# Index-score products of a sparse attention sent in fours over four PSUM banks instead of in twos over two

## The chip, the cores and the metric

The kernel runs on one core of one Trainium2 chip. The metric is the device time of one execution in microseconds (us); lower is better. The engines are TensorE (PE; PEld is its weight load), VectorE (DVE), ScalarE (ACT), GpSimd (POOL) and SyncE (SP, which only issues DMAs). They run their own instruction streams in order and meet at semaphores.

## The reference

One decoder layer on 512 tokens of width 2048 in float32: retention heads beside sparse attention, then an MLP, with norms and conditioning around them. The change touches only the indexer of the sparse attention, which scores every key for every query and keeps the best 128:

```python
h = _modulate(_rms_norm(x, norm1_g), shift1, scale1)
proj = h @ w_in                      # rq, rk, rv, rg, dq, dk, dv, iq, ik, iw
...
s = jnp.einsum('bqhd,bsd->bqhs', qib, k_idx)            # 16 index heads of 64, one shared key
score = jnp.einsum('bqhs,bqh->bqs', jax.nn.relu(s), wb)  # weighted sum over the heads
score = jnp.where(causal, score, -jnp.inf)
_, idx = lax.top_k(score, topk)
```

The query is taken in blocks of 128 tokens. Block 0 needs no choice. Blocks 1, 2 and 3 see 256, 384 and 512 keys.

## The kernel before

**Chunks.** Every large product of the layer is a stream of chunks, numbered q. A chunk is 24 TensorE products of 128 rows by 512 columns (`product`, L1196; three products of split operands for each of eight places). Its weights come by DMA in units of four chunks. ScalarE writes the high half of a chunk's weights (`w_hi`, L514) and GpSimd the low half (`w_lo`, L739), four chunks ahead. Chunks 24 to 27 are `features_chunk`, whose rows read `pj<-h,w_hi` (the moving operand is named first); from chunk 28 on they are `tokens_chunk`, whose rows read `pj<-w_hi,h` and which goes through four token blocks `tb`, six products each.

**Index items.** There are 48 items, one for each query block (1, 2, 3) and index head; items 0 to 23 are the first eight heads, 24 to 47 the last eight. Eight items in a row have the same width: 256, 384, 512 columns, then again. Item n is worked on by three engines in turn:

- TensorE: one small product of 64 rows (L1413, `pa<-ikT,iqT`; the trace shows two weight loads and two matmuls for each) into bank n % 4 of the PSUM tensor `pa`. Even heads lie in partitions 0 to 63 and odd ones in 64 to 127.
- ScalarE: relu out of the bank into one of two halves of the SBUF tile `stage` (`index_relu`, L606). It waits until item n - 2 has been added, since that used the same half.
- VectorE: multiplies by the head's weight and adds to `score` (`index_item`, L924 for head 0 of a block and L927 for the others).

**Where the items stand.** `INDEX_ITEMS` says how many items go with chunk 24, 25, and so on, up to chunk 33: 6, 6, 6, 6, 4, 4, 4, 4, 4, 4. On TensorE they stand inside the chunk, in twos: in a features chunk behind the second, fourth and seventh of its eight places; in a tokens chunk behind the first and the third token block. A two waits until the item four places before its second one has been taken out of its bank (`need(pe, idx_taken, n - 2)`).

**What else runs there.** On VectorE the items of chunk q stand ahead of a piece of another job, `ada_add` (L1013 and L1015: four linked operations of 512 columns on rows that a DMA brings; the accumulator is `part_rows` or `ada_acc`). From chunk 30 on rounds of the top-k search (L937, L938) stand between. On ScalarE the relus of chunk q + 1 stand behind the split of chunk q + 4 and, in chunks 24 to 27, behind the copy of an `iqT` tile (L550) that the last eight heads need (`iq_ready`). After chunks 26 and 30 TensorE sums an accumulator (`later_mod`, L1276); the one after chunk 30 goes to bank 3 of `pa` and so waits for all items that have been sent.

Of the kernel before, what the change touches and what calls it, by code (L numbers as in the profile page):

```python
# [82 lines left out]
Q_TOPK = 30  # L83
ROUNDS = (2, 2, 2, 2, 3, 4, 3, 3, 2, 3, 3, 3, 3, 3, 3, 3, 4)
Q_INDEX = 24
INDEX_ITEMS = (6, 6, 6, 6, 4, 4, 4, 4, 4, 4)

Q_ADA = 16
ADA_SUMS = 16
# [12 lines left out]
def need(eng, sem, value):  # L102

    if isinstance(value, int) and value <= 0:
        return
    eng.wait_ge(sem, value)
# [20 lines left out]
def build(nc, x, vecs, b_ada, consts, w_ada, w_in, w_out, w_mlp1, w_mlp2, out):  # L127
    base = 16512

    def at(name, offset, shape, dt=F32):  # L130
        return nc.alloc_sbuf_tensor_at(name, shape, dt, offset=base + offset)
# [17 lines left out]
    def small(name, *shape):  # L149
# [46 lines left out]
    first = [at("ada_first0", 12 * 4096, [P, 2048]), at("ada_first1", 14 * 4096, [P, 2048]),  # L196
             at("ada_first2", RC + 4096, [P, 2048]), at("ada_first3", RC + 22528, [P, 2048])]
# [51 lines left out]
    iq_ready, idx_done, idx_taken = sem("iq_ready"), sem("idx_done"), sem("idx_taken")  # L249
# [63 lines left out]
    def span(i):  # L313
        return P * (i + 1)
# [15 lines left out]
    def items_at(q):  # L330
        m = q - Q_INDEX
        return range(sum(INDEX_ITEMS[:m]), sum(INDEX_ITEMS[:m + 1])) if 0 <= m < len(INDEX_ITEMS) else ()

# [28 lines left out]
    with block:  # L362
# [829 lines left out]
        def _(pe):  # L1192
            def product(dst, lhs, rhs, start, stop):

                for n, (a, b) in enumerate(PASSES):
                    last = pe.matmul(dst, lhs[a], rhs[b], start=start and n == 0, stop=stop and n == 2)  # L1196
                return last
# [4 lines left out]
            def tokens_chunk(u, j, k0, is_first, is_last, freed, count, items=()):  # L1202

                pe.wait_ge(lo_done, 4 * u + j + 1)
                for tb in range(NB):
                    if is_first and j == 0 and freed is not None:
                        pe.wait_ge(freed, count + tb + 1)
                    for kk in range(2):
                        kt = k0 + 2 * j + kk
                        cols = slice(512 * kk, 512 * kk + 512)  # L1210
                        last = product(pj[:, tb, :], [h[:, kt, s, P * tb:P * tb + P] for s in (HI, LO)],
                                       [w_hi[:, j, cols], w_lo[:, j, cols]],
                                       is_first and j == 0 and kk == 0, is_last and j == 3 and kk == 1)
                    if is_last and j == 3 and tb < 3:
                        last.then_inc(proj_done, 1)
                    if tb == NB - 1:
                        last.then_inc(chunk_used, 1)
                    if tb % 2 == 0:
                        for n in items[tb:tb + 2]:
                            index_item(n)  # L1220

            def tokens_pair(u, freed, count):
# [13 lines left out]
            def features_chunk(q, src, k0, bank, start, stop, ready=None, count=0, trip=0, items=()):  # L1236

                j = q % 4
                pe.wait_ge(lo_done, q + 1 + 32 * trip)
                for kk in range(8):  # L1240
                    if ready is not None:
                        pe.wait_ge(ready, count + kk + 1)
                    last = product(bank, [w[:, j, P * kk:P * kk + P] for w in (w_hi, w_lo)],
                                   [src[:, k0 + kk, s, :] for s in (HI, LO)], start and kk == 0, stop and kk == 7)
                    if kk == 7:
                        last.then_inc(chunk_used, 1)
                    if kk in (1, 3, 6):
                        first = 2 * (1, 3, 6).index(kk)
                        for n in items[first:first + 2]:
                            index_item(n)  # L1250


# [149 lines left out]
            def index_item(n):  # L1402
                i, hh = ITEMS[n]
                rows = slice(IDX_DIM * (hh % 2), IDX_DIM * (hh % 2) + IDX_DIM)
                if n == 0:
                    pe.wait_ge(ikT_ready, 1)
                    pe.wait_ge(kT_ready, KV)
                if n % 4 == 3:
                    pe.wait_ge(mod_taken, done["bank3"])
                if n % 2 == 0:  # L1410
                    need(pe, idx_taken, n - 2)
                pe.wait_ge(iq_ready, 4 if n < 24 else 8)
                pe.matmul(pa[:, n % 4, 0:span(i)], iqT[rows, hh // 2, P * i:P * i + P], ikT[rows, 0:span(i)],  # L1413
                          start=True, stop=True).then_inc(idx_done, 1)
                done["items"] += 1


            for q in range(Q_IQ, Q_LOOP):
                hf, j = divmod(q - Q_IQ, 4)
                if q == Q_IQ + 3:  # L1420
                    pe.wait_ge(small_taken, 1)
                features_chunk(q, h, 8 * hf, pj[:, j, :], hf == 0, hf == 1, items=items_at(q))
                if q == Q_IQ:
                    pe.wait_ge(small_taken, 1)
                    for tb in range(NB):
                        last = pe.transpose(pa[:, 0, P * tb:P * tb + SMALL], small_rows[0:SMALL, P * tb:P * tb + P],
                                            con[0:SMALL, C_ID:C_ID + SMALL])
                    last.then_inc(small_turned, 1)
                if q == Q_IQ + 2:
                    pe.wait_ge(ik_ready, 8)  # L1430
                    pe.wait_ge(proj_free, 8)
                    for tb in range(NB):
                        last = turn(pa[:, 0, P * tb:P * tb + P], ik2[:, tb].rearrange("p a b -> p (a b)"))
                    last.then_inc(ik_turned, 1)
                for n in ada_sum_at(q):
                    later_mod(n)
# [45 lines left out]
            for q in range(Q_LOOP, Q_WO):  # L1482
                g, r = divmod(q - Q_LOOP, PER_GQ)
                group, hf = r // 8, r % 8 // 4

                if group == 0:
                    freed, count = (v_taken, 4 * g - 4) if g else (iq_ready, 4)
                else:
                    freed, count = proj_free, 8 + 16 * g + 4 * (group - 1)
                if q == Q_LOOP:  # L1490
                    pe.wait_ge(mod_taken, done["mods"])
                if r in (24, 32):
                    tokens_pair(q // 4, freed, count)
                elif r not in (25, 33):
                    tokens_chunk(q // 4, q % 4, 8 * hf, hf == 0, hf == 1, freed, count, items_at(q))
                if r == Q_TURN_AT:
                    q_transposes(g)
                if r in TURNS_AT:
                    p_transposes(4 * g + TURNS_AT.index(r))
                if r in OUTS_AT:  # L1500
                    head_out(4 * g + OUTS_AT.index(r))
                if r in LOGITS_AT:
                    head_logits(4 * g + LOGITS_AT.index(r))
                for n in ada_sum_at(q):
                    later_mod(n)
# [60 lines left out]
            for r in range(32):  # L1566
                half_, t = divmod(r, KT)
                if r == KT:
                    last_head_pair()
                if r in (KT, KT + 1):  # L1570
                    continue
                if r >= 4:
                    pe.wait_ge(added, r - 3)
                if r < 4:
                    pe.wait_ge(v_taken, 4 + r + 1)
                features_chunk(4 * U_WO + r, h, 8 * half_, pj[:, t % 4, :], True, True,
                               yd_ready if r == 0 else None)
                if r < 16:
                    k, odd = divmod(r, 2)
                    if not odd:  # L1580
                        if k > 0:
                            ret_out(k - 1)
                        need(pe, yr_ready, k - 1)
                        ret_turn(k)
                    else:
                        ret_inner(k)
                        if k > 0:
                            ret_back(k - 1)
                if r == 15:
                    ret_out(7)  # L1590
# [136 lines left out]
```

## Time and profile before

| | us |
|---|---|
| median of 3 runs | 2377.06 |
| lowest and highest | 2375.36, 2377.11 |
| the profiled execution, own time | 2375.35 |
| its span in the trace | 2373.5 |

The profile's page shows each engine's busy time over the span, the span in 40 slices, the chain of work that ended last, and the costliest groups of instructions. The index items lie between 201 and 286 us, about one part in 28 of the span.

### The profile page before, as it was taken

The numbers are of one execution on the slowest core, as the hardware profiler recorded it, in microseconds if no ns is written. First come the engines' busy times: TensorE is split into PE (matmuls) and PEld (weight loads), VectorE is DVE, ScalarE is ACT, GpSimd is POOL, SyncE is SP. The second block draws the span as 40 slices with busy tenths as digits, with TensorE's granted clock in tenths as the row PEclk, the third lists the DMA queues.
The fourth block names the chain that finished last, engine by engine and source line by source line (L and its number), as shares of the span: only waits on it lengthen the run. The fifth ranks groups of instructions, "written<-read, shape, count | busy, mean of one in ns | idle before, by whom it ended". The sixth has DMA issues, their size and how long they took to land.

```text
span 2373.5 us, 26660 instructions
## 1 busy us (share of the span) xinstructions
PE 2343.3 (99%) x10778; PEld 1902.1 (80%) x10778; DVE 964.1 (41%) x1360; ACT 644.1 (27%) x891; POOL 973.7 (41%) x414
## 2 busy tenths in 40 slices
PE   7999999999999999999999999999999999999999
PEld 4676688788878888788888888888888888888887
DVE  2249898877876877621121121121121121121121
ACT  4223332323224221321221221221221221221222
POOL 1343343344334334344444444444444444444442
PEclk9999999999999999999999999999999999999999
DMA  9976464578647423222333233223323322332231
GB/s 379 357 278 230 161 211 143 196 273 293 223 146 270 142 89 107 71 107 76 102 107 95 82 106 106 85 92 106 106 73 103 106 98 78 106 106 84 93 129 49
DMA packets 183985, 342.13 MB, mean 144 GB/s; under 512 B 4417, under 2 KB 31332, under 8 KB 183012
## 3 DMA queue, kind: packets, MB, share of 16 engines
q1 hardware_dynamic: 175280, 336.77, 41.4%
q10 hardware_dynamic: 8628, 4.28, 0.6%
q8 instruction: 55, 0.90, 0.2%
q14 instruction: 22, 0.18, 0.0%
HBM read 324.26 MB, written 16.78 MB: 144 GB/s over the span
## 4 chain that ended last, share of the span: by engine, by line
PE 93%; DVE 3%; DMA 2%; ACT 1%; issue 0%; SPq 0%; POOL 0%; ACTq 0%; DVEq 0%
PE pj L1196 56%; PE pa L1196 31%; DMA ada_first<-w_ada_in 2%; PE pa L1200 1%; PE pa L1283 1%; DVE part_rows L1015 1%; PE pa L1454 1%; PE pa L1413 1%; PE pa L1477 1%; DVE h L834 1%; PE pa L1276 1%; DVE relu L830 0%; PE pa L1534 0%; PE pa L1526 0%; DVE score L927 0%
## 5 line engine op out<-in xcount | busy, mean ns | idle before, releaser
L739 POOL TENSOR_TENSOR w_lo<-raw,w_hi 128x1024 fp32r<-128x1024 f32 (+1 forms) x396 | 954.5, 2412 | 1339.9 <-ACT w_hi L514 1339.8
L514 ACT ACTIVATE w_hi<-raw 128x1024 fp32r<-128x1024 f32 (+1 forms) x396 | 416.1, 1054 | 1491.2 <-PE pj L1196 945.7
L1196 PE MATMUL pj<-h,w_hi 128*128 128x512 f32 (+1 forms) x1696 | 526.0, 391 | 2.1 <-POOL w_lo L739 1.6
L1196 PE MATMUL pj<-w_hi,h 128*128 128x512 f32 x1408 | 454.1, 396 | 2.2 <-DVE h L834 1.1
L1196 PEld LDWEIGHTS pj<-h,w_hi 128*128 128x128 f32 (+1 forms) x1696 | 314.6, 187 | 74.5 <-issue 7.2
L1196 PE MATMUL pa<-h,w_hi 128*128 128x512 f32 x1152 | 354.9, 389 | 0.0
L1196 PE MATMUL pj<-h,w_lo 128*128 128x512 f32 (+1 forms) x848 | 330.2, 389 | 0.0
L1196 PEld LDWEIGHTS pj<-w_hi,h 128*128 128x128 f32 x1408 | 264.4, 188 | 74.4 <-issue 14.4
L1196 PE MATMUL pa<-mid,w_hi 128*128 128x512 f32 x1024 | 316.1, 390 | 0.0
L1196 PE MATMUL pj<-mid,w_hi 128*128 128x512 f32 x1024 | 315.8, 390 | 0.0
L1196 PE MATMUL pj<-w_lo,h 128*128 128x512 f32 x704 | 274.4, 390 | 0.0
L1196 PEld LDWEIGHTS pa<-h,w_hi 128*128 128x128 f32 x1152 | 216.2, 188 | 45.0
L1196 PE MATMUL pa<-h,w_lo 128*128 128x512 f32 x576 | 224.1, 389 | 0.0
L1196 PEld LDWEIGHTS pj<-mid,w_hi 128*128 128x128 f32 x1024 | 191.8, 188 | 39.6
L1196 PEld LDWEIGHTS pa<-mid,w_hi 128*128 128x128 f32 x1024 | 191.6, 188 | 39.5
L1196 PE MATMUL pa<-mid,w_lo 128*128 128x512 f32 x512 | 199.3, 389 | 0.0
L1196 PE MATMUL pj<-mid,w_lo 128*128 128x512 f32 x512 | 199.3, 389 | 0.0
L1196 PEld LDWEIGHTS pj<-h,w_lo 128*128 128x128 f32 (+1 forms) x848 | 158.5, 187 | 34.1
L1183 DVE SCALAR_TENSOR_TENSOR resid<-pa,mod,resid 128x512 f32<-128x512 f32 x64 | 48.1, 751 | 304.0 <-PE pa L1196 304.0
L1183 DVE SCALAR_TENSOR_TENSOR resid<-pj,mod,resid 128x512 f32<-128x512 f32 x64 | 47.5, 751 | 276.8 <-PE pj L1196 276.8
L1196 PEld LDWEIGHTS pj<-w_lo,h 128*128 128x128 f32 x704 | 132.3, 188 | 27.4 <-issue 1.7
L1015 DVE SCALAR_TENSOR_TENSOR ada_acc<-ada_rows,csilu,ada_acc 128x512 f32<-128x512 f32 x120 | 132.4, 1103 | 25.9 <-DMA ada_rows<-w_ada_in 22.0
(177 smaller groups left out, 1689.5 us busy)
## 6 DMA issues: line engine op xcount, KB each, us to landing
raw<-w_mlp_in SPq DMA_DIRECT2D x64, 2048.0 KB, 8.5
ada_rows<-w_ada_in SPq DMA_DIRECT2D x64, 1024.0 KB, 5.3
raw<-w_in_in SPq DMA_DIRECT2D x22, 2048.0 KB, 10.0
ada_first<-w_ada_in SPq DMA_DIRECT2D x32, 1024.0 KB, 10.9
raw<-w_out_in SPq DMA_DIRECT2D x8, 2048.0 KB, 8.6
ret<-ret_dram SPq DMA_DIRECT2D x32, 256.0 KB, 3.9
raw<-w_in_in SPq DMA_DIRECT2D x3, 1792.0 KB, 13.0
x_nat<-x_in SPq DMA_DIRECT2D x4, 1024.0 KB, 10.4
```

What stands on the lines that cost most here:

```text
L514: act.activation(split_chunk(w_hi, u, j), raw_chunk(u, j), ACT.Copy).then_inc(hi_done, 1)
L739: pool.tensor_tensor(split_chunk(w_lo, u, j), raw_chunk(u, j), split_chunk(w_hi, u, j).bitcast(F32), ALU.subtract).then_inc(lo_done, 1)
L834: dve.scalar_tensor_tensor(h[:, kt, LO, :], tmp[:, kt % 2, :], mod[:, shift_col + kt:shift_col + kt + 1], h[:, kt, HI, :].bitcast(F32), AL ...
L1015: last = dve.scalar_tensor_tensor(acc[:], ada_rows[b][:, i, :], c_col, acc[:], ALU.mult, ALU.add)
L1183: dve.scalar_tensor_tensor(resid[:, t, :], (pa if v % 2 else pj)[:, j, :], mod[:, 5 * KT + t:5 * KT + t + 1], resid[:, t, :], ALU.mult, AL ...
L1196: last = pe.matmul(dst, lhs[a], rhs[b], start=start and n == 0, stop=stop and n == 2)
L1200: return pe.transpose(dst, src, ident)
L1276: last = pe.matmul(bank[:, m:m + 1], rows[:, P * m:P * m + P], ones[:, 0:1], start=True, stop=True)
L1283: last = pe.matmul(pa[32 * i:32 * i + 32, 3, :], c_wide[:, at_:at_ + 32], src[i], start=sec == 0 and s == 0, stop=sec == 1 and s == 3)
L1413: pe.matmul(pa[:, n % 4, 0:span(i)], iqT[rows, hh // 2, P * i:P * i + P], ikT[rows, 0:span(i)], start=True, stop=True).then_inc(idx_done, 1)
L1454: last = pe.matmul(pa[:, bank, col:col + span(i)], qT[:, j, P * i:P * i + P], kT[:, g, 0:span(i)], start=True, stop=True)
L1477: last = pe.matmul(pa[:, 3, P * kb:], v_nat[:, kb, P * g:P * g + P], pT[:, PT_AT[kb]:PT_AT[kb] + width], start=kb == 0, stop=kb == NB - 1, ...
```

## The change

`INDEX_ITEMS` becomes 4, 8, 4, 8, 4, 4, 4, 4, 4, 4. Items are sent in fours: in a tokens chunk all four behind the first token block; in a features chunk with four items behind the fourth place, and in one with eight items behind the second and the sixth place. Since a four fills all four banks, its first item now waits until every item before it has been taken (`need(pe, idx_taken, n)`), and the other three no longer wait for banks.

```diff
-INDEX_ITEMS = (6, 6, 6, 6, 4, 4, 4, 4, 4, 4)
+INDEX_ITEMS = (4, 8, 4, 8, 4, 4, 4, 4, 4, 4)
...
-                    if tb % 2 == 0:
-                        for n in items[tb:tb + 2]:
+                    if tb == 0:
+                        for n in items:
                             index_item(n)
...
-                    if kk in (1, 3, 6):
-                        first = 2 * (1, 3, 6).index(kk)
-                        for n in items[first:first + 2]:
+                    if len(items) == 8 and kk in (1, 5):
+                        for n in items[kk - 1:kk + 3]:
+                            index_item(n)
+                    if len(items) == 4 and kk == 3:
+                        for n in items:
                             index_item(n)
...
-                if n % 2 == 0:
-                    need(pe, idx_taken, n - 2)
+                if n % 4 == 0:
+                    need(pe, idx_taken, n)
```

On TensorE in chunk 25, before: the last two items of 256 columns (6 and 7), four rows of the chunk's products, and the first two of 384 columns (8 and 9).

```order
L1413 MATMUL pa<-ikT,iqT 128x256 x2
L1196 MATMUL pj<-h,w_hi 128x512 x2
L1196 MATMUL pj<-h,w_lo 128x512
L1196 MATMUL pj<-h,w_hi 128x512 x2
L1196 MATMUL pj<-h,w_lo 128x512
L1413 MATMUL pa<-ikT,iqT 128x384 x2
```

The same place after the change: items 4 to 7, four places of products, items 8 to 11.

```order
L1415 MATMUL pa<-ikT,iqT 128x256 x4
L1196 MATMUL pj<-h,w_hi 128x512 x2
L1196 MATMUL pj<-h,w_lo 128x512
L1196 MATMUL pj<-h,w_hi 128x512 x2
L1196 MATMUL pj<-h,w_lo 128x512
L1196 MATMUL pj<-h,w_hi 128x512 x2
L1196 MATMUL pj<-h,w_lo 128x512
L1196 MATMUL pj<-h,w_hi 128x512 x2
L1196 MATMUL pj<-h,w_lo 128x512
L1415 MATMUL pa<-ikT,iqT 128x384 x4
```

Two items stand together where four do now, and twice as many products lie between one group and the next.

On VectorE, in chunks 24 and 25 (the scores of 256 columns, then the `ada_add` of chunk 24 on `part_rows`, then the scores of chunk 25), with - for before and + for after:

```order
 L924 TENSOR_SCALAR score<-stage,w_idx 128x256
-L927 SCALAR_TENSOR_TENSOR score<-stage,w_idx,score 128x256 x5
+L927 SCALAR_TENSOR_TENSOR score<-stage,w_idx,score 128x256 x3
 L1013 TENSOR_SCALAR part_rows<-ada_rows_77,csilu 128x512
 L1015 SCALAR_TENSOR_TENSOR part_rows<-ada_rows_77,csilu,part_rows 128x512 x3
-L927 SCALAR_TENSOR_TENSOR score<-stage,w_idx,score 128x256 x2
+L927 SCALAR_TENSOR_TENSOR score<-stage,w_idx,score 128x256 x4
```

The scores of items 4 and 5 stood ahead of the `ada_add` and now stand behind it.

## Rows read from the trace of the kernel before

**Rows 1.** The page: busy time, share of the span, instructions.
```profile
PE 2343.3 (99%) x10778; PEld 1902.1 (80%) x10778; DVE 964.1 (41%) x1360; ACT 644.1 (27%) x891; POOL 973.7 (41%) x414
```

**Rows 2.** Waits between 200 and 290 us: total, times, longest.
```profile
ACT stage L606 <- DVE score L927: 28.8, 19, 4.2
PE pa L1413 <- ACT iqT L550: 1.1, 1, 1.1
```

**Rows 3.** Chain that ended last, around 237 us: start, us, what.
```profile
218.10 0.76 DVE part_rows L1015
...
234.97 0.76 DVE score L927
...
235.82 0.60 ACT stage L606
...
237.26 0.59 ACT iqT L550
...
237.99 0.70 PE pa L1413 x4
```

**Rows 4.** Timeline of TensorE: start, us, operation, [idle before <- releaser].
```profile
200.31 0.39 PE L1196 MATMUL pj<-h,w_lo 128*128 128x512 f32 x1
...
200.99 0.39 PE L1196 MATMUL pj<-h,w_lo 128*128 128x512 f32 x1
201.30 0.70 PE L1413 MATMUL pa<-ikT,iqT 64*128 64x256 f32 x4
201.94 0.72 PE L1196 MATMUL pj<-h,w_hi 128*128 128x512 f32 x2
202.50 0.40 PE L1196 MATMUL pj<-h,w_lo 128*128 128x512 f32 x1
...
211.55 0.92 PE L1413 MATMUL pa<-ikT,iqT 64*128 64x384 f32 x4
212.40 0.72 PE L1196 MATMUL pj<-h,w_hi 128*128 128x512 f32 x2
...
227.56 1.13 PE L1413 MATMUL pa<-ikT,iqT 64*128 64x512 f32 x4
228.62 0.73 PE L1196 MATMUL pj<-h,w_hi 128*128 128x512 f32 x2
...
258.82 1.02 PE L1276 MATMUL pa<-con,part_rows 128*128 128x1 f32 x8 [0.16 <-issue]
```

**Rows 5.** Timeline of TensorE, narrow products of another job, several in a row.
```profile
69.32 1.07 PE L1283 MATMUL pa<-ada_first,c_wide 128*32 128x512 f32 x8
...
90.88 1.93 PE L1283 MATMUL pa<-ada_first,c_wide 128*32 128x512 f32 x16
...
110.80 3.64 PE L1283 MATMUL pa<-ada_first,c_wide 128*32 128x512 f32 x32
```

**Rows 6.** Timeline of VectorE.
```profile
206.40 0.35 DVE L924 TENSOR_SCALAR score<-stage,w_idx 128x256 f32<-128x256 f32 x1
206.85 2.84 DVE L927 SCALAR_TENSOR_TENSOR score<-stage,w_idx,score 128x256 f32<-128x256 f32 x5
209.60 0.48 DVE L1013 TENSOR_SCALAR part_rows<-ada_rows,csilu 128x512 f32<-128x512 f32 x1
...
214.43 1.07 DVE L927 SCALAR_TENSOR_TENSOR score<-stage,w_idx,score 128x256 f32<-128x256 f32 x2
...
227.31 5.12 DVE L1015 SCALAR_TENSOR_TENSOR part_rows<-ada_rows,csilu,part_rows 128x512 f32<-128x512 f32 x4
232.34 0.15 DVE L808 TENSOR_TENSOR mod<-pj,bias_cols 128x4 f32<-128x4 f32 x1
232.41 5.03 DVE L927 SCALAR_TENSOR_TENSOR score<-stage,w_idx,score 128x512 f32<-128x512 f32 x6
...
274.85 1.61 DVE L927 SCALAR_TENSOR_TENSOR score<-stage,w_idx,score 128x512 f32<-128x512 f32 x2 [2.15 <-ACT stage L606]
```

**Rows 7.** Timeline of ScalarE.
```profile
207.43 0.39 ACT L606 ACTIVATE stage<-pa 128x256 f32<-128x256 f32 x1 [0.21 <-DVE score L927]
...
208.60 0.39 ACT L606 ACTIVATE stage<-pa 128x256 f32<-128x256 f32 x1 [0.20 <-DVE score L927]
```

**Rows 8.** Stretches: us, busy time by engine, granted clock, DMA share, GB/s.
```profile
10.00:20.00 10.00, 5.90 (x46) 2.75 (x44) 1.71 (x10) 5.22 (x9) 0.00 (x0) 1.00 1.06 393
20.00:30.00 10.00, 7.18 (x33) 5.45 (x34) 0.00 (x0) 5.02 (x7) 0.00 (x0) 0.53 1.02 402
60.00:70.00 10.00, 7.76 (x45) 4.47 (x49) 0.00 (x0) 0.40 (x1) 3.07 (x2) 1.00 1.05 387
290.00:345.00 55.00, 55.00 (x260) 45.97 (x259) 52.53 (x105) 21.46 (x54) 26.85 (x11) 1.00 0.45 155
```

## The prediction

> **What bounds the kernel now.** I first read the busy times of the page: TensorE works for 99% of the span [rows 1]. So any time that the change takes off TensorE's stream, or puts into it, is time of the kernel, unless another engine takes it back. Then I read the waits in the stretch of the index items. TensorE stands still only once there for another engine's copy, 1.1 us before item 24 [rows 2]. ScalarE's relus, though, wait 28.8 us in 19 pieces for VectorE's scores. The chain that ended last says why this matters: from 218 to 238 us it hardly touches TensorE. It runs over VectorE's `ada_add` and its scores, the last relus of items 20 to 23, the copy of the `iqT` tile, and only then TensorE's item 24 at 237.99 [rows 3]. VectorE works there with hardly a gap from 206.4 us on [rows 6]. So two engines are near the limit in this stretch: TensorE, and VectorE a little behind it. TensorE passes only because it is allowed to run ahead of VectorE by up to four items.
>
> **What a two costs, and what a four would.** Three products of 512 columns take 0.68 us (200.31 to 200.99), 0.228 each. From the product at 200.99 to the one at 202.50 are 1.51 us with three products and one two of 256 columns: the two costs 1.51 - 0.68 = 0.83 us. Of that the two itself holds 0.64 us (201.30 to 201.94); the other 0.19 us are a late start and a slow first product behind it. A two of 384 columns holds 0.85 us and one of 512 holds 1.06 us [rows 4]; with the same 0.19 they cost 1.04 and 1.25. Eight of each: 8 x (0.83 + 1.04 + 1.25) = 25.0 us.
>
> The trace of before shows no four of this shape. The slope of the three rows is 0.42 us for 256 columns; a second two that simply streams on would add its columns alone: 0.43, 0.64, 0.85 us. The nearest row that has several groups in a row is the narrow product of the conditioning job: 8 matmuls last 1.07 us, 16 last 1.93, 32 last 3.64, so each further group of 512 columns adds 0.86 us [rows 5]. This agrees with 0.85, so I take it. A four then gives back 0.40 us over two twos, and twelve fours give back 12 x 0.40 = **4.8 us** (bounds: 0 if the second two pays as much as the first, 12 x 0.4 if it streams on).
>
> **What the new wait costs.** A four waits until every earlier item is out of its bank. An item is out when ScalarE has done its relu, and that needs the score of the item two before. I went through the stretch with these steps: relu 0.39 us at 256 columns [rows 7] and some 0.5 and 0.6 at 384 and 512; score 0.57, 0.70, 0.84 us from one to the next (2.84/5; 5.03/6); `ada_add` 4.8 to 5.1 us (209.60 to 214.43; 5.12) [rows 6].
>
> First stop, chunk 25. Chunk 24 starts at 199.85 (six products before 201.30). It holds 24 products and one four (0.83 + 0.43), so it ends at 206.6, 1.2 us earlier than before because two items less are in it. Items 4 to 7 come 6 products later at 208.1; item 3 was taken at 207.8 [rows 7], so no wait. The four costs 1.26 us less its lead-in, twelve products 2.74, and TensorE wants items 8 to 11 at 212.0. VectorE has scored items 0 to 3 at 208.5. Its `ada_add` follows at once and lasts to 213.5. Only then comes the score of item 4 (to 214.1), which lets relu 6 go; after the score of item 5, relu 7 goes at 214.7 and is done at 215.1. TensorE stands still for **3.1 us**. Before, items 8 and 9 needed only that item 5 was out of its bank, which it was at 209.0 [rows 7], 2.5 us ahead of them [rows 4].
>
> Second stop, chunk 27, the same with 512 columns. TensorE wants items 20 to 23 at 232.3. VectorE has got back part of its lag and ends the `ada_add` of chunk 26 at 231.8; the scores of 16 and 17 and the relu of 19 end at 233.9: **1.6 us**.
>
> Third stop, item 24 in chunk 28. It exists already, 1.1 us [rows 2, 3]. The relus of items 20 to 23 start only when the late four is in its banks; VectorE ends its scores some 1.7 us later than before, and the `iqT` copy comes at 239.7 instead of 237.9. But TensorE too is later and wants it at 238.9: **0.8 us**, 0.3 less than before.
>
> In the tokens chunks 28 to 33 a four stands behind the first six products, one whole chunk (7 us) after the last. Items 28 and 32 are wanted at about 246.6 and 253.4, and the relus before them end 0.5 and 0.0 us earlier: no wait, but nothing to spare at the second. What is late next is the sum behind chunk 30, which takes bank 3 and waits for items 34 and 35. Before it waited 0.16 us [rows 4]. Now VectorE ends the `ada_add` of chunk 29 at about 258.3, relu 35 ends at 260.3, and TensorE wants the bank at 259.1: **1.2 us**. Behind it the `w_hi` and `w_lo` work is four chunks ahead and hides there. SyncE's queue keeps its order; its loads of `ada_rows` and weights wait for VectorE and GpSimd by at most the same 2 us, and no wait of TensorE in this stretch is for them.
>
> **The sum.** Saved: 4.8. New stops: 3.1 + 1.6 + (0.8 - 1.1) + (1.2 - 0.2) = 5.4. Net **+0.6 us**. The same hand calculation run on the order of before gives TensorE's rows to 0.3 us throughout, so I trust its differences to about 1 us. If the second two in a four saved nothing, three of the stops would shrink to 2.5, 1.0 and 0.5 us and the last would be gone, and the net would be about +1.5. The stops give way where TensorE is slower; that is what it means that VectorE sets the pace. Against the profiled execution's own 2375.35 us the sum is 2376.0; the median of the runs shown lies 1.7 higher, at 2377.06, and gives **2377.6**.
>
> The Trainium skill bears on this from two sides. TensorEngine Tiling (Array Packing), Key Properties, says that changing the tiling mode drains TensorE, which is the 0.40 us that a four saves; by that rule alone the time would be 2372.3. The same page, under PSUM Bottleneck, says that tiling speeds up TensorE but not the emptying of PSUM, which may become the bottleneck. By that rule the gain stays with the engines that empty the banks, and the 28.8 us of relus waiting for scores already show it here.
>
> **The rivals.**
>
> A: *the gain comes through.* If the fours seldom waited, 4.8 us would go, 2377.06 - 4.8 = 2372.3. For it: every item's wait is satisfied early from chunk 31 on, where VectorE waits up to 2.15 us for relus [rows 6]. Against it: at chunk 25 the order on VectorE puts a 5 us `ada_add` between the scores of items 3 and 4, whatever the exact durations. To come out at 0, that wait would have to end 3 us sooner. And behind the items VectorE is busy 52.5 of 55 us up to 345 [rows 8], so it would take back part of an early arrival. Half a gain (2374 to 2375) is likelier than the whole.
>
> B: *the stop costs the clock.* TensorE's granted clock fell to 0.53 in the stretch from 20 to 30 us, the level of 1.2 GHz, after a stretch in which it was busy 5.9 of 10 us; after 7.76 busy of 10 it stayed at 1.00 [rows 8]. In the new kernel some 3.1 us of idle come in one piece near 212 us. If the clock then fell for as long as it did there, products would take twice as long for some 10 us and 5 us would be lost: 2377.6 + 5 = 2382.6, slower. It decides only if the stop at 212 us is as good as the sparse work ahead of 20 us; against it speaks that the stretch from 60 us has 2.2 us of idle and kept its clock, and that TensorE is full on both sides of the stop. The Trainium skill, in TensorE: Matmul & The Clock Gate (Why this matters for your kernels), warns of the clock falling back after an idle gap between bursts of matmuls, so the risk is to be counted.
>
> C: *the fours do not run as one.* The weight loads of the second two wait for the first, nothing is saved, and the stops remain: +1.5 to +2 us, 2378.8. The narrow products speak against it.
>
> **How the numbers follow.** The forecast, stops and savings that nearly cancel (-1.5 to +2.5 us), has 0.72. C has 0.10. A has 0.08 in its full form and 0.04 in the half form. B has 0.06. Faster or slower by 0.2% means below 2372.3 or above 2381.8; about so much can be told from no change by a measurement of this kernel. A's full form lies at the edge, so faster gets 0.06. Slower gets B and a small part for stops that are longer than I think, 0.09. The same: 0.85. The range takes the forecast, the half form of A and C, and the scatter of 1.7 us that the runs of before show: 2374.2 to 2380.6.
>
> **What would show it.** In the trace after: L1415 with 8 matmul rows together, lasting about 1.1, 1.6 and 2.0 us; TensorE idle some 3 us before item 8 near 212 us, 1.6 near 232, under 1 near 239, and about 1 before the sum after chunk 30; 48 items ended at about the same time as before, near 282 us; TensorE's clock at 1.00 there. The forecast is wrong if the wait near 212 is under 2 us with the others gone (A), or if the clock row there is under 1 (B). It would also be wrong if something behind 290 us moved by more than 1 us, which I do not expect.

## The result, and the profile after

| | before | after |
|---|---|---|
| median, us | 2376.76 (6 runs) | 2394.88 (6 runs) |
| lowest and highest | 2375.36, 2377.11 | 2391.32, 2397.76 |
| profiled execution, own time | 2375.35 | 2397.76 |
| its span | 2373.5 | 2396.0 |

The change makes the kernel slower: 1.0074 times before, with an interval of 1.0064 to 1.0085. That is 18.1 us where 0.6 were forecast, far outside the range of 2374.2 to 2380.6.

The page of the kernel after: the busy time of the engines, and the queue that brings the instructions (packets, MB, share of the DMA engines' span). The first row answers to [rows 1]; the queue's row in the page of before is 55 packets and 0.90 MB.

```profile
span 2396.0 us, 26649 instructions
PE 2351.9 (98%) x10778; PEld 1913.1 (80%) x10778; DVE 953.5 (40%) x1360; ACT 644.0 (27%) x891; POOL 977.0 (41%) x414
q8 instruction: 100, 1.64, 0.3%
```

TensorE has as many matmuls as before, 8.6 us more busy time and 22.5 us more span. So it stands still more, and runs slower in places. The waits of TensorE between 200 and 290 us, in the kernel after (total, times, longest), beside [rows 2]:

```profile
PE pa L1415 <- ACT stage L606: 4.1, 2, 2.7
PE pa L1278 <- ACT stage L606: 1.4, 1, 1.4
PE pa L1415 <- ACT iqT L550: 0.7, 1, 0.7
PE pa L1415 <- DVE mod L808: 0.6, 1, 0.6
```

The first three rows are the four stops of the prediction. The last one was not in it. But all this is 6.8 us of standing still, against 1.3 in before, and the fours save 4.8 of work. The larger part of the 22.5 us is far away, in the MLP. Its steps are a loop in TensorE's own stream: six passes, with a jump back after each of the first five. The waits of TensorE between 1000 and 2390 us, in the kernel after:

```profile
PE pj L1196 <- issue: 8.5, 5, 2.0
```

The kernel before has no such row there. "Issue" is time in which the engine waits for nothing that the profile shows. The timeline of TensorE in the kernel after, around the first and the third of the five stops (start, duration, what, [idle before <- releaser]):

```profile
1324.52 0.61 PE L1196 MATMUL pj<-h,w_hi 128*128 128x512 f32 x2
1324.97 0.39 PE L1196 MATMUL pj<-h,w_lo 128*128 128x512 f32 x1
1325.20 0.39 PE L1196 MATMUL pj<-h,w_hi 128*128 128x512 f32 x1
1327.27 0.50 PE L1196 MATMUL pj<-h,w_hi 128*128 128x512 f32 x1 [1.69 <-issue]
1327.61 0.39 PE L1196 MATMUL pj<-h,w_lo 128*128 128x512 f32 x1
...
1679.18 0.51 PE L1196 MATMUL pj<-h,w_hi 128*128 128x512 f32 x1 [1.75 <-issue]
1679.52 0.40 PE L1196 MATMUL pj<-h,w_lo 128*128 128x512 f32 x1
1679.75 0.62 PE L1196 MATMUL pj<-h,w_hi 128*128 128x512 f32 x2
1680.22 0.41 PE L1196 MATMUL pj<-h,w_lo 128*128 128x512 f32 x1
1680.44 1.03 PE L1196 MATMUL pj<-h,w_hi 128*128 128x512 f32 x2
1681.27 0.63 PE L1196 MATMUL pj<-h,w_lo 128*128 128x512 f32 x1
```

Four products of a chunk are issued and then nothing for 1.7 us, and no wait for weights, operands or banks shows. This comes once behind each of the five jumps. Behind the third stop a pair of products soon lasts 1.03 us instead of 0.61: the clock has fallen. The stretch of 3.4 us there (busy of PE, PEld, DVE, ACT, POOL, then the granted clock, DMA share, GB/s):

```profile
1680.00:1683.40 3.40, 3.40 (x10) 2.67 (x9) 0.00 (x0) 0.00 (x0) 0.00 (x0) 0.57 0.64 176
```

So the 22.5 us of the two spans divide into:

- the part with the loop, from one and the same product (the 4667th matmul of the trace, at 998 us here and at 991 in before) to the last small products of the output: 15.2 us (five stops, 8.5; three stretches of 3.4 us at half clock, at 1680.5, 1857.9 and 2035.4 us, which lose 1.7 each; the remaining 1.6 are not taken apart),
- the index section, from the first product of chunk 24 to the 876th product (L1196) of the trace, near 310 us: 111.86 us instead of 109.02, so 2.84,
- 4.5 us elsewhere: chunk 24 starts 2.8 us later, before any changed row, and one stretch at half clock lies near 967 us. Both come and go in the profiles of other kernels below, whatever their order of items.

### The profile page after: what moved, and what is told of

The parts are those of the page before. It is cut to its first block, busy times and chain, and to the rows that moved or that the text cites. A ratio compares the mean times of both kernels' runs of the same rounds, so it can differ in the third digit from the quotient of the medians.

```text
span 2396.0 us, 26649 instructions
## 1 busy us (share of the span) xinstructions
PE 2351.9 (98%) x10778; PEld 1913.1 (80%) x10778; DVE 953.5 (40%) x1360; ACT 644.0 (27%) x891; POOL 977.0 (41%) x414
## 3 DMA queue, kind: packets, MB, share of 16 engines
q8 instruction: 100, 1.64, 0.3%
## 4 chain that ended last, share of the span: by engine, by line
PE 91%; DVE 5%; DMA 2%; issue 1%; ACT 0%; SPq 0%; POOL 0%; ACTq 0%; DVEq 0%
PE pj L1196 54%; PE pa L1196 31%; DVE part_rows L1015 1%; DMA ada_first<-w_ada_in 1%; DVE ada_acc L1015 1%; PE pa L1200 1%; PE pa L1285 1%; DMA ada_rows<-w_ada_in 1%; PE pa L1456 1%; DVE score L927 1%; PE pa L1479 1%; DVE h L834 0%; DVE relu L830 0%; PE pa L1278 0%; DMA rows<-vecs 0%
## 5 line engine op out<-in xcount | busy, mean ns | idle before, releaser
L1196 PE MATMUL pj<-h,w_hi 128*128 128x512 f32 (+1 forms) x1696 | 530.8, 394 | 10.5 <-issue 8.5
L1196 PE MATMUL pj<-w_hi,h 128*128 128x512 f32 x1408 | 454.4, 397 | 1.8 <-DVE rot L965 1.4
L1196 PEld LDWEIGHTS pj<-h,w_hi 128*128 128x128 f32 (+1 forms) x1696 | 317.1, 188 | 83.4 <-issue 15.1
L1196 PE MATMUL pa<-h,w_hi 128*128 128x512 f32 x1152 | 355.0, 389 | 0.0
L1196 PE MATMUL pj<-h,w_lo 128*128 128x512 f32 (+1 forms) x848 | 332.0, 392 | 0.0
L1196 PEld LDWEIGHTS pj<-w_hi,h 128*128 128x128 f32 x1408 | 265.8, 189 | 71.7 <-issue 12.5
L1196 PE MATMUL pa<-mid,w_hi 128*128 128x512 f32 x1024 | 316.2, 390 | 0.0
L1196 PE MATMUL pj<-mid,w_hi 128*128 128x512 f32 x1024 | 315.9, 390 | 0.0
L1196 PE MATMUL pj<-w_lo,h 128*128 128x512 f32 x704 | 275.6, 392 | 0.0
L1196 PEld LDWEIGHTS pa<-h,w_hi 128*128 128x128 f32 x1152 | 216.2, 188 | 45.1
L1196 PE MATMUL pa<-h,w_lo 128*128 128x512 f32 x576 | 224.1, 389 | 0.0
L1196 PEld LDWEIGHTS pj<-mid,w_hi 128*128 128x128 f32 x1024 | 191.9, 188 | 39.6
L1196 PEld LDWEIGHTS pa<-mid,w_hi 128*128 128x128 f32 x1024 | 191.6, 188 | 39.5
L1196 PE MATMUL pa<-mid,w_lo 128*128 128x512 f32 x512 | 199.3, 389 | 0.0
L1196 PE MATMUL pj<-mid,w_lo 128*128 128x512 f32 x512 | 199.3, 389 | 0.0
L1196 PEld LDWEIGHTS pj<-h,w_lo 128*128 128x128 f32 (+1 forms) x848 | 159.7, 188 | 34.5
L1196 PEld LDWEIGHTS pj<-w_lo,h 128*128 128x128 f32 x704 | 133.1, 189 | 27.8 <-issue 1.7
L1015 DVE SCALAR_TENSOR_TENSOR ada_acc<-ada_rows,csilu,ada_acc 128x512 f32<-128x512 f32 x120 | 126.9, 1058 | 30.2 <-DMA ada_rows<-w_ada_in 26.4
```

The lines of the kernel that those rows point to most:

```text
L1015: last = dve.scalar_tensor_tensor(acc[:], ada_rows[b][:, i, :], c_col, acc[:], ALU.mult, ALU.add)
```

## The experiments

Two questions: what stops the loop, and why the index section costs 2.8 us and not 0.6. Unless it is said otherwise a ratio is against the kernel before, run on the same chip.

**What stops the loop.** The one thing that the change moves there is the place of the code. Half of the bank waits of the items went, from 22 instructions to 11, and TensorE's stream has 14,240 instructions instead of 14,251; the page's total went from 26,660 to 26,649. The instructions come in packets of 16 KB (1.64 MB in 100). Theory: a packet is a piece of code, TensorE keeps a few pieces, and where the loop's start lies among their edges decides if the loop stays or must be fetched again in each pass. Rival: the fours in the index section do it, by something that they leave behind.

**e1, the fours with the code at its old place.** The missing waits are put back behind the fours' first wait, where they are met at once.

```diff
                 if n % 4 == 0:
                     need(pe, idx_taken, n)
+                if n % 4 == 2:
+                    need(pe, idx_taken, n - 2)
```

> Theory P (place of the code): the change removed 11 wait instructions from TensorE's stream ahead of the MLP loop (14,251 to 14,240 in all), and with the loop 11 instructions earlier its body is fetched anew in every pass. This kernel is the changed one with 11 redundant waits back in (the third item of each four waits for what the first has waited for), so the loop stands where it stood before. By P the five waits of 1.2 to 2.0 us in the MLP loop are gone, instruction fetches are 55 packets again on the queue that shows 100 in the changed kernel, and the time is 2376 to 2382 us; the stops of the fours near 217, 236, 242 and 263 us stay. Rival C (the clock): the stops near 217 us shift the clock's state and all later falls of it follow; then the time stays near 2394. Rival D (data): the MLP's loads come late after the fours; then it stays near 2394 too, with the waits still there.

**e2, the twos with the code moved.** The kernel before; odd items, all but item 3, no longer wait on `iq_ready`, which the even item ahead has done. 11 instructions go with it.

```diff
-                pe.wait_ge(iq_ready, 4 if n < 24 else 8)
+                if n % 2 == 0 or n == 3:
+                    pe.wait_ge(iq_ready, 4 if n < 24 else 8)
```

> The kernel before, items in twos as before, with 11 instructions fewer ahead of the loop: odd items no longer repeat the wait for the iqT tile (which the even item ahead has done). By P the waits in the MLP loop appear, 100 fetch packets instead of 55, and the time is 2388 to 2396 us although nothing in the index items is different. By C and D it stays at 2377.

Measured: e1 2381.89 us (10 runs; before 2376.94), 1.0019 [1.0009, 1.0028], and 55 packets of instructions. e2 2392.26 us (4 runs), 1.0058 [1.0041, 1.0075], and 100 packets. The waits of TensorE in e2, from 1000 us on:

```profile
PE pj L1196 <- issue: 8.8, 5, 2.0
```

With the index section of before and 11 instructions less, the loop stops five times. With the fours and the 11 put back, it doesn't: from the 4667th matmul to the output it takes 1378.7 us in e1 and in before, 1393.9 in after and 1394.9 in e2. The rival falls. Of the 18.1 us about 13 to 15 are the place of the code (after less e1, 13.0; e2 less before, 15.3), and about 5 are the fours.

**e3, e4, e5: other places.** Waits that are long met are added to the stream of before, ahead of the loop: 100, 220 and 245 instructions. e9 is the kernel after with 111 more, that is 100 past the place of before.

```diff
+            spare = {"left": 100}    # 220 in e4, 245 in e5, 111 in e9
...
+                        if kk == 1 and u >= 9 and spare["left"] > 0:
+                            spare["left"] -= 1
+                            pe.wait_ge(const_landed, 32)
+                            pe.wait_ge(rows_landed, 32)
```

> The kernel before with 100 instructions more ahead of the loop (satisfied waits, one in each token block of later chunks). If what counts is how many fetch pieces of 256 instructions the loop's 1,598 touch, and the kernel before starts it just behind an edge, it still touches 7 here: 55 to 56 packets and 2377 us. If the kernel before is only fast at exactly its own place, it is slow, 2390.

> The same with 220 more. The loop then starts 220 to 231 instructions into a piece and touches 8 pieces: about 100 packets and 2388 to 2396 us. If it stays at 2377 with 56 packets, the count of pieces touched isn't the rule and only fewer instructions hurt.

> The kernel before with 245 instructions more ahead of the loop. Read from the runs so far: the stop comes where the jump back lands just ahead of the edge of a fetch piece of 256 instructions, so that only some 11 instructions arrive with the first piece and TensorE waits for the next. 245 more is 11 fewer and one whole piece, so the loop lies towards the pieces as in the changed kernel. By this theory five waits of 1.6 to 2.3 us, about 101 packets and 2388 to 2396 us, the same as with 11 fewer. If it stays at 2377 like the 220 more did, it is not the place within a piece but something else that fewer instructions do.

> The changed kernel, fours and all, with 111 instructions more ahead of the loop (100 more than the kernel before has). By the same theory 55 to 56 packets, no wait in the loop, and the time of the padded fours: 2380 to 2384 us. What is left over the kernel before is then the stops of the fours (about +0.6 net by the prediction's sum) and what TensorE's clock loses behind them; in its profile each stretch at 0.50 behind a stop should account for 1.7 us per 3.4 us. If the clock doesn't fall at all in the profile, that profile's span should be within 1.5 us of the kernel before's, counted from item 0 on.

| kernel | instructions against before | packets | stops in the loop | median, us | ratio, interval |
|---|---|---|---|---|---|
| e3 | +100 | 56 | 0 | 2376.93 | 0.9998 [0.9988, 1.0007] |
| e4 | +220 | 101 | 0 | 2377.97 | 1.0005 [0.9995, 1.0014] |
| e5 | +245 | 101 | 5, and one of 0.2 us | 2391.76 | 1.0055 [1.0035, 1.0075] |
| after | -11 | 100 | 5 | 2394.88 | 1.0074 [1.0064, 1.0085] |
| e9 | -11 + 111 | 56 | 0 | 2382.57 | 1.0019 [1.001, 1.0029] |

e5, e9 and e3 came as expected; e4 did not. It has no row of waits on issue behind 1000 us, but its instruction queue is as busy there as in the kernel after. The queues of e4 between 1300 and 2300 us (before has 5 packets there, after 49):

```profile
q8 instruction: 50, 0.82, 0.3%
```

The waits of TensorE in e5, from 1000 us on (the sixth lasts 0.2 us and lies behind the last jump, ahead of its stop):

```profile
PE pj L1196 <- issue: 8.9, 6, 1.9
```

So the theory was half right, and e4 mends it. The stream of before divided by its packets is 14,251 / 55 = 259 instructions each; 256 fits every row of the table. The loop has 1,598 instructions (1,597 are recorded from one jump to the next), 6.2 pieces. Where it begins at an edge (before) or 100 past it (e3, e9) it touches 7 pieces, and nothing is fetched again. Where it begins 11 ahead of an edge (after, e2; e5, since 256 - 245 = 11) or 36 ahead of one (e4, 256 - 220) it touches 8, and nine pieces are fetched in each of five passes: 55 + 45 = 100.

In the instruction records the jump itself lasts 3.3 to 3.7 us in after and 3.4 to 3.8 in e4, against 0.21 to 0.24 in before; the products that are queued cover it. Then the piece at which it lands matters. In e4 it still holds 36 instructions, and the next piece arrives nearly in time: e4 has no stop, and its part from the 4667th matmul on is 0.8 us longer than in before. In after it holds 11: three register and wait instructions and the four products of the timeline above, a weight load and a matmul each. They are as many as the change removed, so in before the loop begins right at an edge.

The packets of the queue show the rest. Behind the first jump of after (1320.56 us) the first packet starts at 1321.48, the jump ends at 1323.91, the second packet starts at 1324.62 and ends at 1325.95, and the stop ends at 1327.27. Behind all 15 such jumps of after, e2 and e5 the stop ends 1.2 to 1.5 us after the end of the second packet. So TensorE stands still until the next piece has come. The stop needs both: a loop over too many pieces, and a jump to the end of one.

The Trainium skill (Runtime: NRT & Kernel Launch, Instruction fetch mechanics) says that "Branching breaks sequential prefetch": a taken branch to a target that is not held makes the engine fetch it before it can go on. The trace agrees, with its jumps of 3.3 us and more and its stops of 1.2 to 2.0 us. The page also gives blocks of 16 KiB, 256 instructions, and 2048 instructions for TensorE, and the packets of 16 KB and the shifts of e4 and e5 fit the 256. But it says as well that only two such blocks are held at a time. There the measurement differs: in before the jump goes back over more than six pieces and nothing is fetched. That 7 pieces stay, and 8 don't, is this case's.

**What the fours cost.** e1 and e9 have no stop in the loop and are the fours as changed. Both are 0.19% slower, 4.5 to 5 us. The timelines of e1: TensorE's fours of 384 columns, the products behind chunk 30's sum, and VectorE's two rows that release the stop.

```profile
216.21 2.46 PE L1417 MATMUL pa<-ikT,iqT 64*128 64x384 f32 x8 [2.75 <-ACT stage L606]
...
264.15 1.55 PE L1417 MATMUL pa<-ikT,iqT 64*128 64x384 f32 x6
267.90 1.65 PE L1417 MATMUL pa<-ikT,iqT 64*128 64x384 f32 x2 [2.20 <-DVE mod L808]
```

```profile
264.53 3.25 DVE L1015 SCALAR_TENSOR_TENSOR ada_acc<-ada_rows,csilu,ada_acc 128x512 f32<-128x512 f32 x4
267.69 0.15 DVE L808 TENSOR_TENSOR mod<-pa,bias_cols 128x4 f32<-128x4 f32 x1
```

The second TensorE row is items 36 to 38 (two matmuls each), the third is item 39 alone. Item 39 goes to bank 3, and bank 3 holds the sum behind chunk 30 until VectorE has copied it (`mod_taken`, L808). On VectorE this copy stands behind an `ada_add`. In before items 38 and 39 stood half a chunk later. VectorE's and TensorE's rows there:

```profile
265.04 0.16 DVE L808 TENSOR_TENSOR mod<-pa,bias_cols 128x4 f32<-128x4 f32 x1
265.08 1.08 PE L1413 MATMUL pa<-ikT,iqT 64*128 64x384 f32 x4
```

The TensorE row is both items; item 39 begins within it at 265.51. The copy ended at 265.20, 0.3 us ahead of it, and left no wait. The fours ask for it half a chunk sooner and stop for 2.2 us. The windows of e1 show what else there is:

```profile
210.00:220.00 10.00, 7.25 (x29) 4.34 (x26) 8.16 (x12) 3.76 (x10) 2.39 (x1) 0.84 1.05 392
...
260.00:270.00 10.00, 6.40 (x25) 3.62 (x24) 9.01 (x19) 3.71 (x7) 2.39 (x1) 0.90 0.46 126
270.00:280.00 10.00, 10.00 (x34) 6.83 (x33) 2.91 (x8) 2.22 (x4) 2.35 (x1) 0.76 0.22 86
```

A granted clock of 0.84 over 10 us is one stretch of 3.4 us at half clock, from 216.7 us, right behind the stop of 2.75 us; 0.90 and 0.76 together are two such stretches from 267.9 us on, right behind the stop of 2.20. That is rival B of the prediction. Two theories for the 5 us: the missed stop, which then is worth 2.2 us and the fall behind it; or rather the first stop and the fall behind that.

**e10, the first stop filled.** e1, with 12 more products ahead of item 8's wait, which compute nothing that is used, so that TensorE doesn't stand still there.

```diff
+                if n == 8:
+                    pe.wait_ge(iq_ready, 5)
+                    fill(12)
                 if n % 4 == 0:
```

> The padded fours with 12 more products of 128 columns on a free bank right ahead of the four that stops near 216 us (items 8 to 11). They compute nothing that is used and only keep TensorE busy for about 2.6 us of the 2.75 us stop. Theory: it is the idle of the stop that lets the clock fall behind it, near 215 us, which cost 1.7 us in one profile and 3.4 us in the other. Then the clock stays at 1.00 from 210 to 230 us here, items 8 to 11 start at the same distance from item 0 as before, and the time is 1.5 to 3.5 us under the padded fours' 2382, 2378.5 to 2380.5 (the fall near 268 us, behind another stop, stays). Rival: the clock falls for another reason, such as the narrow 64-row products of a four, and falls near 215 us all the same; then the time stays at 2381 to 2383.

**e11, the four of chunk 31 half a chunk later**, behind its third token block, where items 38 and 39 stood before.

```diff
-                    if tb == 0:
+                    if tb == (2 if 4 * u + j == 31 else 0):
```

> The padded fours with one four moved: the one of chunk 31 (items 36 to 39) stands behind the third token block instead of the first. In four profiles of fours its last item stopped TensorE, 2.2 us where the clock hadn't already made it late, because it goes to bank 3, where the sum behind chunk 30 lies until VectorE has copied it, and that copy stands behind an ada_add. This stop is missing in the prediction's sum. Here the item is wanted 2.8 us later, so the stop should be gone, the work of the index section should come within 1 us of the twos' (net of the clock), and the clock should not fall near 268 us. Against the padded fours' 2382: 2.2 us for the stop and 1.5 to 2 on average for the clock, 2378 to 2379. If it stays at 2381 or more, the stop only hid the time of another wait.

The timeline of TensorE in e10:

```profile
212.44 2.84 PE L1341 MATMUL pj<-con 128*128 128x128 f32 x24
215.35 1.56 PE L1420 MATMUL pa<-ikT,iqT 64*128 64x384 f32 x8
```

The filling lasts 2.84 us and the four behind it 1.56, so the clock stayed up (1.00 from 210 to 220 us). The code stands 48 instructions further on than in before, with 56 packets and no stop in the loop. Yet e10 took 2382.02 us, 1.0021 [1.0012, 1.0031], no less than e1. In its profile the index section is 4.4 us longer than before, and e1's 6.3; the two have one fall of 3.4 us behind item 39 in e10 and two there in e1. So the fall near 216 us cost e1 next to nothing: TensorE comes later, and the next stop, which VectorE's pace sets and which lasts 1.3 us in e10, is gone. Counted from the start of chunk 24, item 24 begins 0.3 us later in e1 than in e10. A longer fall is not taken up whole: in e9 it lasts 6.8 us there, and item 24 is 1.5 us later. Both the expectation (2378.5 to 2380.5) and its rival (no change of the clock) missed.

e11 took 2377.85 us, 1.0002 [0.9993, 1.0011]. Its waits in the index section:

```profile
PE pa L1417 <- ACT stage L606: 3.3, 2, 2.7
PE pa L1278 <- ACT stage L606: 1.4, 1, 1.4
PE pa L1417 <- ACT iqT L550: 0.7, 1, 0.7
```

The first three stops and the sum's are still there, and the one for `mod` is gone. There is no fall near 268 us, as expected, but there is one of 3.4 us from 263.0, behind the sum's stop. The kernel is 4 us faster than e1 (2381.89), by where one group of four items stands. The first theory holds.

**e6, e7, e8, e12: even chunks.** The first stop comes from the chunk of eight. These kernels have four items with every chunk from 24 on, in fours (e6, e8 and e12 on e1, e7 on before in twos), and the rounds of the top-k search begin a chunk later: none in chunk 30, three instead of two in 31 and 32. In e8 and e12 chunk 32 has eight, four behind its first and four behind its third token block.

```diff
-ROUNDS = (2, 2, 2, 2, 3, ...
+ROUNDS = (0, 3, 3, 2, 3, ...
-INDEX_ITEMS = (4, 8, 4, 8, 4, 4, 4, 4, 4, 4)
+INDEX_ITEMS = (4, 4, 4, 4, 4, 4, 4, 4, 4, 4, 4, 4)      # e6; e7 the same, on before
+INDEX_ITEMS = (4, 4, 4, 4, 4, 4, 4, 4, 8, 4, 4)         # e8, and e12 with e11's line
```

> Fours with the 11 redundant waits (14,251 instructions, the loop as before), but four items in each of twelve chunks (24 to 35) instead of 4, 8, 4, 8, and the top-k rounds from chunk 31 on (0, 3, 3, 2 instead of 2, 2, 2, 2), since they need 32 items. No features chunk has two fours, so by the theory of the stops the waits before items 8 and 20 go to under 0.5 us; some 1.8 us stay before item 28 and 1.5 before the sum after chunk 35. Against the kernel before: -1.9 us by the hand calculation, 2375.0, and no fall of the clock in the stretch, since no stop is over 2 us. If the clock falls all the same, 2376 to 2379.

> The control for the even fours: the same four items in each of twelve chunks and the same top-k rounds, but in twos with the kernel before's own waits (14,251 instructions). By the hand calculation +0.2 us against the kernel before, 2377.1. The difference to the even fours, 2.1 us, is what grouping in fours gives net of its waits; in the traces a four should hold 0.40 us less than two twos.

> As the even fours, but chunks 32, 33 and 34 take 8, 4 and 4 (behind the first and the third token block), so that the sum after chunk 35 waits for nothing. -2.9 us against the kernel before, 2374.0, with waits of 1.8 us before item 28 and 0.6 before item 44. If the rounds of top-k are what ends later and the logits wait, it is no better than the even fours.

> The even fours with 8 at chunk 32 (2378.2), with the same move of chunk 31's four. The stop of 2.0 us before item 31 should go; one of 2.3 us before the sum behind chunk 30 stays. Net of the clock 2.5 us under the twos: 2374.5; with a fall of the clock behind the stop that stays, about 2376. If it comes under 2375, fours do pay.

| kernel | median, us | ratio, interval | index section against before, us | falls of the clock in it |
|---|---|---|---|---|
| e6 | 2380.47 | 1.0017 [1.0008, 1.0026] | +4.9 | 10.2 us from 255.4, 3.4 from 299.8 |
| e7 (twos) | 2376.57 | 1.0000 [0.9991, 1.0009] | -0.1 | none |
| e8 | 2378.18 | 1.0005 [0.9996, 1.0014] | +1.0 | 3.4 from 259.4 |
| e12 | 2375.48 | 0.9992 [0.9983, 1.0001] | -1.3 | 3.4 from 257.5 |

e6 missed its expectation (2375.0, or 2376 to 2379 with a fall), on the side of the clock: its 13.6 us at half clock lose 6.8 us, and the +4.9 without them are the -1.9 that were expected. The first stop did go in all three of the fours (none is over 0.4 us ahead of 250 us), but the sum behind chunk 30 now stops TensorE for longer. The waits of e12:

```profile
PE pa L1279 <- ACT stage L606: 2.3, 1, 2.3
PE pa L1418 <- ACT stage L606: 1.1, 4, 0.4
```

And its window shows the fall behind that stop, 0.88 over 10 us:

```profile
250.00:260.00 10.00, 7.69 (x33) 6.08 (x32) 9.51 (x11) 1.71 (x3) 3.85 (x2) 0.88 0.34 108
```

e12 is the best kernel of the study, 1.5 us under before (2377.02, 21 runs beside it), and its interval still reaches over 1. Whether it beats before is not settled. Without its fall of 3.4 us at half clock (1.7 us) the -1.3 of its index section would be -3.0, an estimate of what the fours would give with the clock kept; it is worked out, not measured. e8 has the four of chunk 31 where e6 has it and waits 2.0 us for the copy in L808; that stop and the fall behind it are its miss (2374.0 expected). e7 shows that even chunks alone, in twos, change nothing.

## Why the prediction was wrong

**The step that failed first** is the sentence that nothing behind 290 us would move by more than 1 us, and with it a sum over the index section alone. It counted what the change does to the fours' time and left out what it does to the length of the stream: 11 wait instructions fewer, none of which costs any time itself. They move the code of the loop, which runs from about 1146 us on, from the edge of a piece of code to 11 instructions ahead of one. In place of no change behind 290 us the runs showed nine pieces fetched again in each of five passes, with a stop of 1.2 to 2.0 us in each: 13 to 15 of the 18.1 us (e1, e2). The risk could have been seen: the page of before has a queue that brings instructions in 55 packets, and the changed kernel has a shorter stream ahead of a loop. What could not be read from it is that the loop lay exactly at an edge. No rival covered this, and all of their times lay within 6 us of the forecast.

**The saving** was right. The fours last 1.13, 1.56 and 1.99 us, as the prediction had them to 0.05 us. The timeline of TensorE in the kernel after:

```profile
205.48 1.14 PE L1415 MATMUL pa<-ikT,iqT 64*128 64x256 f32 x8
210.85 1.13 PE L1415 MATMUL pa<-ikT,iqT 64*128 64x256 f32 x8
217.67 1.56 PE L1415 MATMUL pa<-ikT,iqT 64*128 64x384 f32 x8 [2.75 <-ACT stage L606]
...
230.20 1.99 PE L1415 MATMUL pa<-ikT,iqT 64*128 64x512 f32 x8
236.50 1.99 PE L1415 MATMUL pa<-ikT,iqT 64*128 64x512 f32 x8 [1.33 <-ACT stage L606]
242.17 1.13 PE L1415 MATMUL pa<-ikT,iqT 64*128 64x256 f32 x8 [0.73 <-ACT iqT L550]
...
262.90 1.02 PE L1278 MATMUL pa<-con,part_rows 128*128 128x1 f32 x8 [1.38 <-ACT stage L606]
```

C, that the fours don't run as one, fell. That the 0.40 us that each saves are a drain, as the prediction took them, no run here shows. The prediction's sum for fours that save nothing is wrong too: stops of 2.5, 1.0 and 0.5 and none before the sum are 2.5 + 1.0 - 0.6 - 0.2 = +2.7 us and not +1.5; nothing but C's price rests on it.

**The four stops** came where they were put: 2.75 us near 217 (3.1 forecast), 1.33 (1.6), 0.73 (0.8) and 1.38 before the sum (1.2). The cause is the one given, an `ada_add` between the scores of items 3 and 4, and ScalarE's relu waiting behind it. VectorE and ScalarE in the kernel after:

```profile
209.66 1.66 DVE L927 SCALAR_TENSOR_TENSOR score<-stage,w_idx,score 128x256 f32<-128x256 f32 x3
211.24 0.48 DVE L1013 TENSOR_SCALAR part_rows<-ada_rows,csilu 128x512 f32<-128x512 f32 x1
211.76 4.40 DVE L1015 SCALAR_TENSOR_TENSOR part_rows<-ada_rows,csilu,part_rows 128x512 f32<-128x512 f32 x3
```

```profile
216.65 0.38 ACT L606 ACTIVATE stage<-pa 128x256 f32<-128x256 f32 x1 [4.04 <-DVE score L927]
217.24 0.38 ACT L606 ACTIVATE stage<-pa 128x256 f32<-128x256 f32 x1 [0.20 <-DVE score L927]
```

A, that the gain comes through, fell with them.

**A fifth stop was missed**, 2.2 us before item 39 (e1, e9, e10). The prediction followed the wait for banks (`idx_taken`) through chunk 31, and stopped at the sum; the wait for `mod_taken`, in the line above the changed one, was not followed. With it the sum would have been about +2.8, which is what the index section shows without falls that count (+2.7 to +2.9 in after, e1 and e10; e9's +5.95 less 1.7 and 1.5 for its falls is +2.7). Without that stop e11 shows +0.5, or -0.4 if the 0.8 us are taken off too by which its first fall made item 24 late, against a forecast of +0.6. In the profile of after this stop is only 0.62 us, since a fall of the clock from 263.9 us had made TensorE late already.

**B was given too little**, 0.06. Granted clocks of 0.50 stood behind stops in the index section of every profile with fours, and of none of the six with twos (before, e2, e3, e4, e5, e7). It did not look as B had it: 3.4 us at a time, mostly, so 1.7 us and not 5; behind the first stop (e1, e9, e11) largely taken up by the next ones; and dear behind the last stops, where nothing takes it up. By this sum, an estimate, it is the rest of the 5 us: 5 - 2.8 = 2.2 us, 1.3 falls on average. The same clock takes 5 of the loop's 15 us. The Trainium skill's warning (TensorE: Matmul & The Clock Gate, Why this matters for your kernels) of the clock falling back behind an idle gap was weighed and put low. The clock did fall here. But the page speaks of longer gaps than the stops of 1.1 to 2.8 us behind which it fell, and there the runs differ from it.

## What to carry to other kernels

An edit that adds or removes a few instructions ahead of a loop also moves the loop's code, and that alone was worth 0.6% here with no visible connection: compare the packets of the instruction queue before and after, look for stops on "issue" behind the jump, and repeat the edit with the length of the stream held (spare waits) before judging it. When work is drawn together and asks for its buffers sooner, follow every wait of every item, the unchanged ones too: the wait that was met 0.3 us ahead before is the one that stops the engine. A stop of an engine that another one paces costs less than it seems ahead of a later stop and more than it seems behind the last, where a fall of the clock comes on top.

## What was not expected of the hardware, and what stays open

- A loop of 1,598 instructions on TensorE was kept over 7 pieces of 16 KB and fetched again in every pass over 8. The jump took 0.2 us in the one and 3.3 to 4.0 in the other. With only 11 instructions left in the piece at which it lands it stopped TensorE for 1.2 to 2.0 us each pass; with 36 all five passes together lost 0.8 us. Where between the two the stop begins was not tried.
- The clock fell behind stops of 2.2 to 2.8 us, but also near 263 us behind one of 1.4 (after, e11) and in e6 from 299.8 us, 2.1 us behind one of 1.1, and not behind 2.75 us near 217 in the kernel after, while the same stop in e1, e9 and e11 had it. In the loop it fell behind eight stops of 1.6 to 2.0 us and not behind seven of 1.2 to 1.9. Why one stop brings it and its like doesn't stays open.
- Two differences between profiles were left as scatter: chunk 24 starting up to 2.9 us later, and a fall near 962 to 968 us, in after, e4, e7, e8, e9 and e10 but not in the other profiles. The kernel's own runs differ by as much.
